# Grouped attention's probabilities turned through DRAM and VectorE instead of TensorE, gate sums moved to the mixer A passes, and some orders

## The reference

```
h   = rms_norm(x, g_norm) * (1 + scale) + shift        # shift, scale, gate from silu(c) @ w_ada
z   = h @ w_in                                         # q, k, v, gate of mixer A and mixer B
A   : softmax(q1 k1) - lam * softmax(q2 k2), @ v        # 8 heads, differential attention
B   : softmax(q k) @ v                                  # 8 query heads, 2 key/value heads, grouped
out = x + gate * (concat(norm(A) * silu(ga), B * silu(gb)) @ w_out);  y = rms_norm(out, g_final)
```

## Time and profile before

| | us |
|---|---|
| median of three runs | 1248.04 |
| profiled execution | 1251.43 |
| its span | 1249.6 |
| PE busy in the span | 1209.0 (97%) |
| DVE, ACT, POOL busy | 825.1, 595.2, 258.1 |
| mean granted TensorE clock | 0.995 |

### The profile page before, as it was taken

One profiled execution on the slowest core, in us unless ns is written; L12 is line 12 of the kernel. 1 busy time (PEld: TensorE's weight loads), 2 busy tenths in 40 slices (PEclk: granted clock), 3 DMA queues, 4 the chain that ended last, 5 costly groups with the idle time before them and its releaser, 6 DMA issues.

```text
span 1249.6 us, 16738 instructions
## 1 busy us (share of the span) xinstructions
PE 1209.0 (97%) x6083; PEld 977.5 (78%) x6083; DVE 825.1 (66%) x1270; ACT 595.2 (48%) x1268; POOL 258.1 (21%) x439
## 2 busy tenths in 40 slices
PE   5899999999999999999999999999998999999996
PEld 4455788888888888888888888888887878878885
DVE  4455488677586776766656575665657674789774
ACT  5422325645555465555555464555555656312223
POOL 1211033012031030222222221222223322110111
PEclk9999999999999999999999999999999999999999
DMA  9999232222221232343433334243445523656544
GB/s 351 372 378 350 85 110 77 64 71 74 77 93 47 68 106 51 101 135 108 130 117 120 117 104 143 90 141 96 135 129 162 179 68 110 244 186 227 186 134 177
DMA packets 150642, 178.46 MB, mean 143 GB/s; under 512 B 10544, under 2 KB 113616, under 8 KB 149792
## 3 DMA queue, kind: packets, MB, share of 16 engines
q1 hardware_dynamic: 136688, 131.63, 32.4%
q0 software_dynamic: 13424, 45.20, 11.6%
q10 hardware_dynamic: 448, 0.57, 0.1%
HBM read 155.19 MB, written 22.17 MB: 142 GB/s over the span
## 4 chain that ended last, share of the span: by engine, by line
PE 89%; DVE 4%; SPq 3%; DMA 2%; issue 1%; ACT 1%; POOL 0%; DVEq 0%; POOLq 0%; ACTq 0%
PE z_ps L753 24%; PE z_ps L755 23%; PE z_ps L754 23%; PE ring L844 4%; PE ring L935 4%; SPq L684 2%; PE ring L878 2%; PE ring L877 2%; PE ring L779 2%; PE ring L939 2%; DVE gate_acc L1775 1%; DMA ada_raw<-in_w_ada_dram 1%; PE ring L754 1%; PE ring L755 1%; PE ring L942 1%
## 5 line engine op out<-in xcount | busy, mean ns | idle before, releaser
L753 PE MATMUL z_ps<-w_hi,xt_hi 128*128 128x512 f32 x1350 | 550.5, 408 | 2.7 <-issue 1.1
L755 PE MATMUL z_ps<-w_hi,xt_lo 128*128 128x512 f32 x1350 | 528.1, 391 | 0.0
L754 PE MATMUL z_ps<-w_lo,xt_hi 128*128 128x512 f32 x1350 | 527.6, 391 | 0.0
L1058 ACT ACTIVATE w_hi<-w_raw 128x512 fp32r<-128x512 f32 x270 | 169.6, 629 | 350.0 <-PE z_ps L755 316.5
L753 PEld LDWEIGHTS z_ps<-w_hi,xt_hi 128*128 128x128 f32 x1350 | 254.6, 189 | 70.5 <-issue 27.0
L1511 DVE TENSOR_TENSOR w_lo<-w_raw,w_hi 128x512 fp32r<-128x512 f32 x270 | 195.5, 727 | 166.4 <-ACT w_hi L1058 165.9
L755 PEld LDWEIGHTS z_ps<-w_hi,xt_lo 128*128 128x128 f32 x1350 | 254.0, 188 | 55.5
L754 PEld LDWEIGHTS z_ps<-w_lo,xt_hi 128*128 128x128 f32 x1350 | 255.3, 189 | 41.0
L1612 DVE TENSOR_REDUCE small<-s_sb 128x2 f32<-128x1536 f32 (+1 forms) x60 | 88.0, 1467 | 20.5 <-ACT s_sb L1058 20.5
L1223 ACT ACTIVATE s_sb<-s_sb,small 128x768 f32<-128x768 f32 (+1 forms) x120 | 98.0, 820 | 3.5 <-DVE small L1612 3.5
L1983 POOL TENSOR_TENSOR sg<-sg,zs 128x128 f32<-128x128 f32 (+1 forms) x60 | 37.9, 632 | 267.3 <-DVE sg L1581 266.7
(11 more groups left out here) (197 smaller groups left out, 1359.2 us busy)
## 6 DMA issues: line engine op xcount, KB each, us to landing
w_raw<-in_w_in_dram SPq DMA_DIRECT2D x188, 256.0 KB, 3.2
ada_raw<-in_w_ada_dram SPq DMA_DIRECT2D x64, 512.0 KB, 11.3
w_raw<-in_w_out_dram SPq DMA_DIRECT2D x64, 256.0 KB, 3.9
gate_raw<-in_w_ada_dram POOLq DMA_DIRECT2D x12, 1024.0 KB, 8.3
p_spill<-s_sb SPq DMA_DIRECT2D x28, 384.0 KB, 2.3
p_blocks<-p_spill SPq DMA_DIRECT2D x112, 96.0 KB, 2.2
w_raw<-in_w_in_dram POOLq DMA_DIRECT2D x20, 256.0 KB, 6.3
o_spill<-row_st POOLq DMA_DIRECT2D x14, 320.0 KB, 3.3
```

Source lines behind the costliest of these rows:

```text
L753: pe.matmul(out, hi_l, hi_r, start=start, stop=False)
L754: pe.matmul(out, hi_l, lo_r, start=False, stop=False)
L755: return pe.matmul(out, lo_l, hi_r, start=False, stop=stop)
L1058: return act.activation(out, in_, ACT.Copy, **kw)
```

## The change

- `by_blocks` holds for tiles 1 to 4 of passes 1 to 11: the 16 G tiles too. Two rows (one for each head) go to DRAM in one DMA and come back in four. DVE turns both (`turn_blocks`), ACT copies each to the high half (`blocks_hi`, at the end of step T), and DVE subtracts (`blocks_lo`, in the step after T, behind that step's `split_w`). V waits for `p_split`. PE's 12 transposes, the four-bank copies and the four subtractions of each such tile go.
- One block buffer (`p_block`, or `p_pair` for G) stands where there were two: the reads of a tile wait until DVE has turned the tile before.
- `turn_blocks` stands ahead of `gated` on DVE.
- Gate block 0 is summed at steps 3, 13 and 15 of passes 6 to 11; `step_gate(0)` and `gate_rows_out(0)` stand at pass 12 step 0, POOL's write of the rows at pass 12 step 3.
- POOL: in pass 12 `load_row` stands behind `o_root`; `gf_b` is loaded at pass 14 step 1 behind the residual, not at pass 13 step 15 ahead of the gate slabs.

```diff
-GATE_EARLY = [9, 11, 13, 15]
+GATE_EARLY = [(D_IT + 1, 13), (D_IT + 1, 15)] + [(D_IT + _p, _s) for _p in (2, 3, 4, 5, 6) for _s in (3, 13, 15)]
...
-    return t > 0 and group_kind(a) == "D" and a < OUT_IT - 1
+    return t > 0 and KV_IT < a < OUT_IT - 1
...
-GATE_LOADS[(G_IT + 1, 1)] = [(0, 0)]
-GATE_SUM_AT[(D_IT + 1, 0)] = GATE_ROWS_AT[(D_IT + 1, 0)] = GATE_OUT_AT[(D_IT + 1, 3)] = 0
+GATE_LOADS[(D_IT + 1, 3)] = [(0, 0)]
+GATE_SUM_AT[(OUT_IT - 1, 0)] = GATE_ROWS_AT[(OUT_IT - 1, 0)] = GATE_OUT_AT[(OUT_IT - 1, 3)] = 0
...
             def move_blocks(a, t):
-                b, n = t % 2, p_count(a, t)
+                b, n = t % 2, TURNED.index((a, t))
                 sp.wait_ge(p_ready, n_step(a, t) + 1)
-                sp.dma_start(p_spill[b], s_sb[:, b, 0, :]).then_inc(p_out[b], 16)
-                if n > 1:
-                    sp.wait_ge(p_turned, turns_before(a, t) - 1)
+                if group_kind(a) == "G":
+                    sp.dma_start(p_spill[b].rearrange("c q n -> q c n"), s_sb[:, b, :, :]).then_inc(p_out[b], 16)
                 else:
+                    sp.dma_start(p_spill[b, 0], s_sb[:, b, 0, :]).then_inc(p_out[b], 16)
+                if n:
+                    sp.wait_ge(p_turned, turns_until(*TURNED[n - 1]))
...
+            def blocks_hi(a, t):
+
+                for c_ in range(2):
+                    act.wait_ge(p_turned, turns_until(a, t) - 1 + c_)
+                    copy(pt_hi[c_], pt_raw[:, c_, 1, :]).then_inc(pt_hi_done, 1)
...
+                for kind, a, t in late:
+                    if kind == "T" and by_blocks(a, t) and group_kind(a) == "G":
+                        blocks_hi(a, t)
...
+            def blocks_lo(a, t):
+
+                for c_ in range(2):
+                    dve.wait_ge(pt_hi_done, PT_BEFORE[(a, t)] + c_ + 1)
+                    dve.tensor_tensor(pt_lo[c_], pt_raw[:, c_, 1, :], pt_hi[c_].bitcast(F32), ALU.subtract).then_inc(p_split, 1)
...
                 old, late = late, steps_at(it, s)
+                for kind, a, t in old:
+                    if kind == "T" and by_blocks(a, t) and group_kind(a) == "G":
+                        blocks_lo(a, t)
...
+                for kind, a, t in late:
+                    if kind == "T" and by_blocks(a, t):
+                        turn_blocks(a, t)
                 if not first:
                     for kind, a, t in old:
                         if kind == "V":
                             gated(a, t)
-                for kind, a, t in late:
-                    if kind == "T" and by_blocks(a, t):
-                        turn_blocks(a, t)
```

More of the change, by code:

```diff
@@ L219 @@
 for _k in range(KT):
[L220 removed]
+    _it, _s = GATE_EARLY[_k]
     GATE_SUMS[(_it, _s)] = (0, [_k])
@@ L358, in build @@
     pt_f, _ = place("pt_f", [P, NKEY], F32, pt0)
-    p_blocks = [place(f"p_blocks{i}", [P, QUAD, KB * SUB], F32, pt0 + 4 * NKEY * (1 + i))[0] for i in range(2)]
+    pt_raw, _ = place("pt_raw", [P, 2, 2, NKEY], F32, pt0)
+    p_block, e0 = place("p_block", [P, QUAD, KB * SUB], F32, pt0 + 4 * NKEY)
+    gate_acc0, e0 = place("gate_acc0", [P, 2, NCOL], F32, e0)
+    gate_raw0, e0 = place("gate_raw0", [P, NCOL], F32, e0)
+    assert e0 <= pt0 + 4 * 4 * NKEY
     v_f, _ = place("v_f", [P, 7, DH], F32, pt0 - 4 * 7 * 2 * DH)
@@ L444, in build @@
         pt_hi_done = sem("pt_hi_done")
-        p_turned = sem("p_turned")
-        p_out, p_in = ([sem(f"{w}{b}") for b in range(2)] for w in ("p_out", "p_in"))
+        p_turned, p_in, p_split = sem("p_turned"), sem("p_in"), sem("p_split")
+        p_out = [sem(f"p_out{b}") for b in range(2)]
         o_part, o_sq, o_rstd, og_ready = sem("o_part"), sem("o_sq"), sem("o_rstd"), sem("og_ready")
@@ L552, in t_parts, with turns_until, wait_row_out @@
             return [(n + 2 * c + j // 4, c, j, m, 0, True) for c in hs for j, m in ((0, 4), (4, 2))]
+        TURNED = [(a, t) for a in range(OUT_IT) for t in range(TILES) if by_blocks(a, t)]
         def p_count(a, t):
-            return 2 * (a - D_IT) + (t - 1) // 2 + 1
-        def turns_before(a, t):
-            return (TILES - 1) * (a - D_IT) + t - 1
+            return sum(u % 2 == t % 2 for _, u in TURNED[:TURNED.index((a, t)) + 1])
+        def turns_until(a, t):
+            return sum(heads(of) for of, _ in TURNED[:TURNED.index((a, t)) + 1])
+        def wait_row_out(eng, a, t):
+            before_it = [(of, u) for of, u in TURNED if u % 2 == t % 2 and (of, u) < (a, t)]
+            if before_it:
+                eng.wait_ge(p_out[t % 2], 16 * p_count(*before_it[-1]))
         def quads(row):
@@ L925, in step_v @@
                     wait_free(pe, m)
-                if by_blocks(a, t):
-                    pe.wait_ge(p_turned, turns_before(a, t) + 1)
+                if by_blocks(a, t) and group_kind(a) == "D":
+                    pe.wait_ge(p_turned, turns_until(a, t))
+                elif by_blocks(a, t):
+                    pe.wait_ge(p_split, turns_until(a, t))
                 bank = claim(n)
@@ L1178, in scores_out @@
                     act.wait_ge(zr_ready, a + 1)
[L1179 to L1185, removed]
+                wait_row_out(act, a, t)
+                if by_blocks(a, t) and group_kind(a) == "D":
                     for c_ in range(2):
@@ L1828, in _ @@
                 if (it, s) == (D_IT + 1, 1):
-                    for n in range(TURN[("T", D_IT - 1, TILES - 1)], TURN[("T", D_IT - 1, TILES - 1)] + 4):
-                        wait_full(dve, n)
+                    wait_full(dve, TURN[("V", D_IT - 1, TILES - 1)])
                     for c_, rows in enumerate(HALVES):
@@ L2121, in _ @@
                 late = [step for step in late if step[0] != "V" or step[2] < TILES - 1]
+                if it == OUT_IT - 1 and s >= ROW_LAG - 1:
+                    load_row(s - (ROW_LAG - 1))
                 if it == OUT_IT and s == 10:
@@ L2124, in _ @@
                     load_gate_rows(0)
-                if it == OUT_IT and s == 15:
+                if it > OUT_IT and s == 1:
+                    load_out_operands(it - OUT_IT)
+                if it == OUT_IT + 1 and s == 1:
                     for u in range(2):
```

48 lines of the change are left out of this document (30 added, 18 removed).

## The result

The changed kernel takes 1255.8 us (median of 6 runs, 1252.7 to 1257.9), the kernel before 1247.9 beside it (6 runs): ratio 1.0065, 95% interval 1.0049 to 1.0081. It is slower by 0.65%, 8 us. The forecast was 1251.0 with 0.46 on slower. The profiled execution took 1257.9, its span is 1256.1, 6.5 more than before.

What follows compares the result with a forecast made beforehand. PE bounds the kernel, busy 1209.0 of 1249.6 us. Terms -23.1 + 32.4 + 6.8 - 4.9 - 6.1 + 1.6 - 3.8 = +2.9 gave 1251.0 against the median 1248.0, range 1242 to 1260.

Steps and rivals of the forecast that it cites:

- PE work removed: G passes: 12 transposes cost 1.45 us a tile; removing them from 16 tiles saves 23.1 us of PE's path.
- New waits of V in G: G passes: V waits on a longer ACT and DVE chain, 8.1 us a pass with refill, 32.4 in four.
- The transfers are late: Rival: turns in G wait for DRAM, 8 to 15 us more, 1259 to 1266; chance 0.08.
- The clock: G passes: granted clock falls to half behind each V4 wait, not behind V3, costing 6.8 us.
- 4 x 1.7: G passes: four clock falls behind V4, each losing 1.7 us of PE, 6.8 in all.
- The 1.85 in the opening: Wait of 1.85 at 47.05 that left the clock at full speed, cited against a fall behind V3.
- D passes: Mixer A: `turn_blocks` ahead of `gated` removes six V waits at t = 1, 0.8 each with refill: -4.9 us.
- gate sums fall where DVE otherwise waits: Steps 3, 13 and 15: sums of about 1.4 us each fall where DVE otherwise waits for ACT's weights, costing nothing.
- Pass 12: V waits and their clock loss go, -6.1 us; O waits for a bank at the start, +1.6.
- -3.5 for the long wait: Pass 12: the V wait of 3.35 us goes, saving 3.5; its clock loss is counted separately.
- Pass 14: `step_gate(1)`'s wait of 1.94 and its clock loss go with `gf_b` behind the slabs: -3.8 us.
- ACT and DVE are earlier: Rival: copy and subtractions in G not behind the next step's `split_w`, 16 us less, 1235; chance 0.13.

Runs made afterwards that it cites:

- experiment 3: The changed kernel with `gated` put ahead of `turn_blocks` on DVE again, as before the change: 1264.7 us, ratio 1.0121.
- 4: The changed kernel with the row loads of pass 12 put ahead of `o_root` on POOL again, as before the change: 1258.9 us, ratio 1.0071.
- experiment 7: The changed kernel with mixer A's gate sums at steps 3, 7 and 15 and step 14's slab loads moved to 8: 1253.8 us, ratio 1.0034.
- kernel 9: The changed kernel with the last `gate_inverse` of a pass behind the turn of t = 1 on DVE, not ahead: 1257.9 us, ratio 1.0070.
- 10: The changed kernel with g_final's load back at step 15 of pass 13, ahead of the gate slabs: 1256.0 us, ratio 1.0051.
- 11: The changed kernel with the first chunk's gate rows made in step 3 of pass 12, not step 0: 1256.3 us, ratio 1.0056.
- experiment 2: The changed kernel with G's `blocks_lo` directly behind `turn_blocks` on DVE, ahead of the next step's w_lo: 1241.7 us, ratio 0.9937.
- experiment 5: The changed kernel with 20 unread transposes of a constant tile on PE before its wait for V4 of each G pass: 1254.5 us, ratio 1.0039.
- kernel 6: On top of experiment 2, G's blocks moved head by head, each write waiting only for its own exponentials: 1231.4 us, ratio 0.9867.

## Why the prediction came out as it did

**PE work removed**, predicted -23.1. A G pass without waits takes 75.1 against 80.6: 5.5 a pass, -22.1 in four. Right.

**New waits of V in G**, predicted +32.4, measured +28.0 by whole passes (26.7 by the idle times). The four places and their order are right, and their sizes: t1 2.0 predicted and 1.7 measured, its half at the score part included; t2 0.3 and 0.2; t3 1.7 and 1.6; t4 3.3 and 3.2. What was mis-sized is the refill, counted at 0.8 a pass on top of starts that already held most of it (7.0 - 6.7 = 0.3 was left), and 0.3 too much at t1. The chain's arithmetic is borne out by taking its parts away: 2.1 us of foreign w_hi and w_lo out of it removed V1 to V3's waits. "The transfers are late" was not true of the change, where no turn in G waits for its blocks, but it was nearer than its 0.08 said: as soon as the chain was 2.1 us shorter, V4's turn waited 1.0 to 1.8 for data. The write took 4.3 us, where I had taken 3.5, and the read 3.7 for 3.0.

**The clock**, predicted +6.8, measured +7.2: it fell behind all four V4 and not behind V3, as forecast. That the two figures are so near is in part luck: one fall was double, and the others cost less than 1.7, since part of them lay in the wait. In the traces of all kernels that kept this wait of 3.0 to 3.5 us (the changed one, 3, 4, 7, 9, 10, 11) it fell 24 times in 28, so my "4 x 1.7" was a likely value and not a sure one; that is much of the 5 us by which runs of the changed kernel differ, their mean clock going from 0.989 at 1256.9 us to 0.995 at 1252.7. The 1.85 in the opening, on which I leaned for "no fall", does not hold either: it did not fall in the kernel before, but behind the same waits of 1.85 and 1.88 it did in experiments 2 and 10.

**G together**: +16.1 predicted, +13.1 measured.

**D passes**, predicted -4.9, measured -3.5. Without the new V4 waits the six passes take 408.9 (experiment 7), 6.3 less than before. Of these, 0.8 are the matmuls of `step_gate(0)`, which left pass 6 for pass 12; the order gave 5.5, 0.9 a pass and not 0.8; and the gate slabs loaded beside the block reads took 2.8 back. That cover I had judged for DVE alone, where "gate sums fall where DVE otherwise waits", and not for the DMA that each sum triggers: that term stood at nothing. This is an error of the prediction that the total hides.

**Pass 12**, predicted -6.1 + 1.6 = -4.5, measured +0.1. This is the step that failed, by 4.6 us, more than the whole 3.6 by which the traced difference missed the forecast. The long V1 wait and its clock did go (experiment 3 has them back, +3.7), and O waits the 1.5 that was reckoned. Wrong was that no V would wait then ("-3.5 for the long wait", "-0.9 for the two small ones"): V1 to V4 wait 0.5, 1.3, 0.6 and 1.6, 3.9 in all where the kernel before had 4.6, so 0.7 was gained and not 4.4. The other 0.8 are the gate's matmuls, which D gave up. The prediction looked only at `gated` in front of the turn, and put at nothing that the row loads now stand behind `o_root` on POOL. In the changed kernel ACT waits 3.3 and 1.2 us for rows ahead of V2 and V3, and with it the exponentials, `combine` and the turn; in the kernel before it waits for no row there. V4's turn waits 1.05 for its blocks. Experiments 4 and 11 changed which V waits, and did not make the pass shorter: blocks late for DVE in the one (2.9 at V3 and at V4), rows late for ACT in the other (3.4 and 3.2). Which resource would have to give is open; all that is shown is that this pass has several limits within 1 to 2 us of each other.

**Pass 14**, predicted -3.8, measured -3.6. The reason given, g_final's load ahead of the slabs, is half borne out: with the load back in its old place the slabs and the weights are late again, but by 2.2 us and not by 4.3, and PE does not wait. So the size came true, and what else made the weights so late before is not known.

The sum by terms of the trace: +13.1 - 3.5 + 0.1 - 3.6 + 0.4 = +6.5 against +2.9. The medians differ by 7.9, since the profiled execution of before lay 3.4 above its median and that of after 2.1.

Of the rivals, the one with 0.13 ("ACT and DVE are earlier") named the remedy, the low part not behind the next `split_w`. That experiment 2 is 16 us faster than the changed kernel, the figure of that rival, is in part luck: the rival counted waits alone, and in the trace some 13 are waits and 4 the clock.

## What to carry to other kernels

Work taken off the bounding engine is worth its length only if the chain that replaces it fits in the slots between; draw the chain instruction by instruction on its in-order engines, and look for another step's work in the middle of it. When a chain is shortened, ask what arrives next: here the transfer lay 1 us behind the chain, and moving it head by head and moving the consumer by two tiles gave 9 and 7 us more, each by itself. A term that comes out right proves nothing of its reason; test it by putting the old part back.

## What the runs showed of the hardware

- The clock is not a fixed price of a wait. It fell behind idle times of 3.0 to 3.5 us in 24 of 28 cases, behind 2.37 and not behind 2.38 us in one trace, behind 1.94 in the kernel before, and never behind those of 1.4 to 1.5 at V3 in 32 cases; but in kernel 9 one fall stands behind two waits of 1.0 and 1.2 us that follow each other within 3 us. The Trainium skill, TensorE: Matmul & The Clock Gate, section HAM oscillation — how this bites in real kernels, sets its limit for idle gaps above the 3.0 us of these waits; the falls behind 3.0, 2.37 and 1.94 do not agree with it, and the measurement decides.
- PE transposes of a constant, 20 in 2.35 us, kept the clock up at all four V4 of the profiled execution, where it otherwise fell behind 24 of 28 (experiment 5).
- A quarter of the blocks, 192 KB for two heads, landed 3.7 us after its issue, and 96 KB for one head in 2.2 (kernel 6). The price of splitting by head were issues on SP, 8 in 3.64 us for 4 in 1.8, and the writes: each head's 384 KB took 4.0 to land in G, two of them in flight, where D's took 2.3 in the changed kernel.
